# GDN inverse with tiles of 32 weight columns, first value tile's taps at the iteration's tail, SSD state groups one step later

## The reference, cut to what matters

```python
# GDN, per pair of value heads that share a query and key head (16 such pairs)
qkv = silu(causal_conv(qkv, conv_buf, conv_w))      # 4 taps per channel
a_mat = (k_beta @ k.T) * decay * strict             # lower triangular, per chunk
t_mat = inverse(eye + a_mat)                        # used for u and w of the chunk
# then: new values, state update, output, rmsnorm(o) * silu(z)

# SSD, per group (8 groups of 8 heads): conv, y_diag, state per chunk, y_off, and for the samples
S = S * exp(dt * A) + outer(x * dt, B);  y = S @ C  # 8 sample states per group
```

## Time and profile before

| what | value |
|---|---|
| time, median of 3 runs (lowest to highest) | 2444.06 us (2442.49 to 2444.54) |
| the profiled execution's own time | 2443.26 us |
| its span, first to last instruction | 2441.5 us |
| mean granted clock of TensorE, share of full | 0.990 |
| PE / DVE / ACT / POOL busy | 96% / 66% / 52% / 72% |
| one iteration of the GDN loop | 63.5 us (L440 at 286.05 and at 349.58) |

### The profile page before, as it was taken

How to read it: one execution, slowest core, us unless ns; L and a number is a source line. 1 busy time by engine, 2 the same in 40 slices (tenths; PEclk the granted TensorE clock), 3 DMA queues, 4 the chain that set the end, 5 groups by cost and what they waited for, 6 DMA issues and landing times.

```text
span 2441.5 us, 58796 instructions
## 1 busy us (share of the span) xinstructions
PE 2346.2 (96%) x21280; PEld 2201.1 (90%) x21280; DVE 1604.1 (66%) x3203; ACT 1260.5 (52%) x2201; POOL 1762.6 (72%) x2236
## 2 busy tenths in 40 slices
PE   5899999999999999999998989999999999999997
PEld 5799999999999999989998978989998999899897
DVE  7667666666666676661217466988898889712374
ACT  4555555555555555543335446555555555433443
POOL 5466566565555555558887968988898889789896
PEclk9999999999999999999999989999999999999998
DMA  5444444444444444436443445766576656554433
GB/s 200 149 156 148 155 155 148 151 142 148 144 155 147 148 143 143 146 114 222 155 164 134 163 152 204 239 202 202 189 240 212 198 193 229 189 182 155 155 136 123
DMA packets 126772, 410.84 MB, mean 168 GB/s; under 512 B 21344, under 2 KB 37984, under 8 KB 122112
## 3 DMA queue, kind: packets, MB, share of 16 engines
q1 hardware_dynamic: 80784, 294.49, 35.3%
q10 hardware_dynamic: 45936, 115.64, 14.0%
HBM read 363.47 MB, written 46.61 MB: 168 GB/s over the span
## 4 chain that ended last, share of the span: by engine, by line
PE 53%; POOL 32%; issue 10%; DVE 3%; ACT 1%; POOLq 0%; DMA 0%; DVEq 0%; ACTq 0%
POOL wl L335 32%; PE psj L358 14%; PE psj L359 12%; PE psj L360 12%; PE psA L393 2%; PE psC L393 2%; PE psE L393 2%; PE psD L504 1%; PE psA L569 1%; PE psC L519 1%; DVE xl L1398 1%; PE psA L382 1%; PE psE L535 0%; PE psE L387 0%; PE psC L387 0%
## 5 line engine op out<-in xcount | busy, mean ns | idle before, releaser
L335 POOL TENSOR_TENSOR wl<-ring,wh 128x256 fp32r<-128x256 f32 x2232 | 1762.4, 822 | 656.2 <-ACT wh L806 651.8
L358 PE MATMUL psj<-xh,wh 128*128 128x288 f32 x4400 | 1358.0, 309 | 37.2 <-DVE xl L1413 17.0
L359 PE MATMUL psj<-xl,wh 128*128 128x288 f32 x4400 | 1305.1, 297 | 0.0
L360 PE MATMUL psj<-xh,wl 128*128 128x288 f32 x4400 | 1300.3, 296 | 0.0
L358 PEld LDWEIGHTS psj<-xh,wh 128*128 128x128 f32 x4400 | 831.4, 189 | 90.9 <-issue 52.7
L806 ACT ACTIVATE wh<-ring 128x1024 fp32r<-128x1024 f32 x558 | 586.1, 1059 | 596.1 <-PE psj L360 556.9
L359 PEld LDWEIGHTS psj<-xl,wh 128*128 128x128 f32 x4400 | 834.2, 190 | 1.9
L360 PEld LDWEIGHTS psj<-xh,wl 128*128 128x128 f32 x4400 | 835.0, 190 | 0.0
L887 ACT ACTIVATE arena<-psj 128x256 f32<-128x256 f32 x112 | 42.8, 383 | 206.7 <-PE psj L360 200.5
L1768 DVE TENSOR_TENSOR h<-h,psj 128x288 f32 x32 | 14.5, 454 | 154.9 <-PE psj L360 154.9
L1839 DVE SCALAR_TENSOR_TENSOR arena<-arena 128x256 f32<-128x256 f32 x144 | 111.3, 799 | 3.4
(11 more groups left out here) (345 smaller groups left out, 2935.5 us busy)
## 6 DMA issues: line engine op xcount, KB each, us to landing
ring<-weights_d SPq DMA_DIRECT2D x558, 512.0 KB, 3.3
h<-gstate_d ACTq DMA_DIRECT2D x16, 1024.0 KB, 6.3
gst_s_d<-h ACTq DMA_DIRECT2D x16, 1024.0 KB, 3.9
h<-sstate_d ACTq DMA_DIRECT2D x32, 512.0 KB, 5.6
sst_s_d<-h ACTq DMA_DIRECT2D x32, 512.0 KB, 4.1
arena<-g_rows_d ACTq DMA_DIRECT2D x16, 864.0 KB, 6.0
arena<-s_rows_d ACTq DMA_DIRECT2D x8, 1152.0 KB, 8.7
h_spill_d<-h ACTq DMA_DIRECT2D x2, 2304.0 KB, 7.2
```

Of the source, the lines that this page charges most:

```text
L335: ins = pool.tensor_tensor(wl[:, s, n:n + 2], ring[:, s, n:n + 2], wh[:, s, n:n + 2].bitcast(F32), ALU.subtract)
L358: pe.matmul(out, w_h, xh[:, kt, :], start=(kt == 0), stop=False)
L359: pe.matmul(out, w_h, xl[:, kt, :], start=False, stop=False)
L360: mm = pe.matmul(out, w_l, xh[:, kt, :], start=False, stop=(kt == KT - 1))
```

## The change

- `blocks` gets the number of weight columns of a product as an argument. For A*D (psC) and for the update of D (psA) it is 32: four products for each matrix, each with 32 weight columns and the same 32 moving columns as before, for 32 rows of the output. For the update of E (psE) it stays 64.
- The prompt taps 0, 1 and 2 of value tile 0 leave the inverse. They are made in `v_first`, behind the norm of the next queries and keys and ahead of the Y writes, after a wait for ScalarE's take of that tile (`took_act` at m * 6 + 11). For the first iteration they are made in the prologue. Tap 0 of value tile 1 goes to the very start of an iteration, ahead of L1544. The other taps move up by one place or more, and `g_convv` is raised ahead of `mask_p(4)`.
- In the 7 iterations of the SSD loop the two groups of state products and the sum go from steps 45, 55 and 70 to 46, 56 and 71. The last iteration stays.

```diff
@@ -80,7 +80,7 @@
 
 SMP_PE = {n: i + 1 for i, n in enumerate(("ast", "sqs", "esp", "smp", "us", "osm"))}
 SMP_ACT = {n: i + 1 for i, n in enumerate(("asc", "kmc", "qs", "vnds"))}
-G_DVE_LINKS, S_DVE_LINKS = 19, 40
+G_DVE_LINKS, S_DVE_LINKS = 16, 40
 S_CONV = ((0, 2), (2, 4), (4, 5), (5, 6))
 ARENA = 15900
 
@@ -387,10 +387,10 @@
                     mm = pe.matmul(bank[r:r + 64, cols], lhsT[:, r:r + 64], rhs, start=True, stop=True)
                 return mm
 
-            def blocks(bank, u, lhsT, rhs, lv):
-
-                for r in (0, 64):
-                    mm = pe.matmul(bank[r:r + 64, u * 32:(u + 1) * 32], lhsT[:, r:r + 64], rhs[:, in_block(r, lv), :],
+            def blocks(bank, u, lhsT, rhs, lv, n):
+
+                for r in range(0, P, n):
+                    mm = pe.matmul(bank[r:r + n, u * 32:(u + 1) * 32], lhsT[:, r:r + n], rhs[:, in_block(r, lv), :],
                                    start=True, stop=True)
                 return mm
 
@@ -455,7 +455,7 @@
                     for u in range(4):
                         D = half(gDE[:, 0], lv, 0)[:, u]
                         if lv < 5:
-                            mm = blocks(psC, u, gAT[:, u, :], D, lv)
+                            mm = blocks(psC, u, gAT[:, u, :], D, lv, 32)
                         else:
                             mm = halves(psC, slice(u * 64, (u + 1) * 64), gAT[:, u, :], D)
                     mm.then_inc(S("g_p"), 1)
@@ -466,12 +466,12 @@
                     pe.wait_ge(S("g_pm"), m * 6 + lv + 1)
                     if lv < 5:
                         for u in range(4):
-                            mm = blocks(psA, u, gDE[:, 1, u, :], half(gP[lv], lv, 0)[:, u], lv)
+                            mm = blocks(psA, u, gDE[:, 1, u, :], half(gP[lv], lv, 0)[:, u], lv, 32)
                         mm.then_inc(S("g_qd"), 1)
                     for u in range(4):
                         E = half(gDE[:, 1], lv, 1)[:, u]
                         if lv < 5:
-                            mm = blocks(psE, u, gP[lv][:, u, :], E, lv)
+                            mm = blocks(psE, u, gP[lv][:, u, :], E, lv, 64)
                         else:
                             mm = halves(psE, slice(u * 64, (u + 1) * 64), gP[lv][:, u, :], E)
                     mm.then_inc(S("g_qe"), 1)
@@ -683,7 +683,7 @@
 
             def ssd_mix(m, e, more):
 
-                at_smp, at_xt, at_states, at_sum = (33, 36, (45, 55), 70) if more else (41, 46, (54, 62), 72)
+                at_smp, at_xt, at_states, at_sum = (33, 36, (46, 56), 71) if more else (41, 46, (54, 62), 72)
                 if e == 20:
                     pe.wait_ge(S("s_cv"), m + 1)
                     pe.wait_ge(S("s_yd"), m + 1)
@@ -1536,8 +1536,22 @@
                 dve.tensor_tensor(gATS[:, :, :], gDTS[0:NS], gR[0:NS, :, 1, SEQ:T], ALU.mult)
                 do.link(dve.tensor_tensor(u4(gAT[:, :, :]), u4(gDT[:, :, :]), beta, ALU.mult))
 
+            def v_tap(i, j, part):
+
+                a, b, at = ((0, SEQ, j), (SEQ, T, UC + DEC_B * j))[part]
+                out = gCR[:, 2 + i, a:b]
+                return dve.scalar_tensor_tensor(out, gU[:, 2 + i, at:at + b - a], gpc_tap[1][:, i, j:j + 1],
+                                                out, ALU.mult, ALU.add)
+
+            def v_first():
+
+                do.link(v_tap(0, 0, 0))
+                do.link(v_tap(0, 1, 0))
+                v_tap(0, 2, 0)
+
             def gdn_body(m, full):
 
+                v_tap(1, 0, 0)
                 dve.wait_ge(S("g_tok"), m + 1)
                 kk = bc(psC[:, 0:256].rearrange("p (c t) -> p c t", c=NC), 2, 2)
                 qk = bc(psC[:, 256:512].rearrange("p (c t) -> p c t", c=NC), 2, 2)
@@ -1559,13 +1573,6 @@
                                             bc(gKN[:, 1 - n, SEQ:T].rearrange("p (t b) -> p t b", b=DEC_B), 1, DEC_B),
                                             bc(seq_mask, 2, DEC_T), ALU.mult)
                 ins.then_inc(S("g_mk"), 1)
-
-                def v_tap(i, j, part):
-
-                    a, b, at = ((0, SEQ, j), (SEQ, T, UC + DEC_B * j))[part]
-                    out = gCR[:, 2 + i, a:b]
-                    return dve.scalar_tensor_tensor(out, gU[:, 2 + i, at:at + b - a], gpc_tap[1][:, i, j:j + 1],
-                                                    out, ALU.mult, ALU.add)
 
                 def parts(lv):
                     return [(slice(r, r + 64), in_block(r, lv)) for r in (0, 64)] if lv < 5 else [(slice(0, P), slice(0, 1))]
@@ -1602,30 +1609,26 @@
                 dve.wait_ge(S("g_e1"), m + 1)
                 do.link(dve.tensor_copy(gU[:, 2:4, UC:US], gpc_cache[1]))
                 mask_p(0)
-                do.link(v_tap(0, 0, 0))
+                v_tap(1, 1, 0)
                 less_q(0)
                 do.link(v_tap(0, 0, 1))
                 mask_p(1)
-                do.link(v_tap(1, 0, 0))
+                v_tap(1, 2, 0)
                 less_q(1)
-                v_tap(1, 0, 1)
-                do.link(v_tap(0, 1, 1))
+                do.link(v_tap(1, 0, 1))
                 mask_p(2)
-                do.link(v_tap(0, 1, 0))
+                v_tap(0, 1, 1)
                 less_q(2)
-                do.link(v_tap(1, 1, 0))
+                do.link(v_tap(1, 1, 1))
                 mask_p(3)
                 dve.wait_ge(S("g_sample_pe"), m * 6 + SMP_PE["sqs"])
                 dve.tensor_tensor(gBS[:, :, :], bc(ident[0:NS, 0:NS], 1, 2),
                                   psD[0:NS, 256:256 + 2 * NS].rearrange("p (j t) -> p j t", j=2), ALU.add) \
                     .then_inc(S("g_bs"), 1)
-                do.link(v_tap(0, 2, 0))
                 less_q(3)
-                v_tap(1, 2, 0)
-                do.link(v_tap(1, 1, 1))
-                mask_p(4)
                 v_tap(0, 2, 1)
                 v_tap(1, 2, 1).then_inc(S("g_convv"), 1)
+                mask_p(4)
                 dve.wait_ge(S("g_sample_pe"), m * 6 + SMP_PE["esp"])
                 dve.tensor_copy(gES,
                                 bc(psD[0:2 * NS, 320:320 + NS], 1, 4)) \
@@ -1708,6 +1711,8 @@
                 states(3)
                 if full:
                     gdn_qk_norm(m + 1)
+                    dve.wait_ge(took_act, m * 6 + 11)
+                    v_first()
                 else:
                     take_out(T_O1, 2)
                 dve.wait_ge(S("g_ont"), m + 1)
@@ -1742,6 +1747,9 @@
             columns(0)
             gdn_prepare(0)
             dve.wait_ge(took_act, 6)
+            do.link(v_tap(0, 0, 0))
+            do.link(v_tap(0, 1, 0))
+            do.link(v_tap(0, 2, 0))
             with dve.Fori(0, GH - 1) as m:
                 do.enter(m, G_DVE)
                 gdn_body(m, True)
```

## The result

| kernel | us, median (lowest to highest) | against before |
|---|---|---|
| before | 2444.1 | |
| the change | 2514.9 (2511.7 to 2519.4) | 1.0294 [1.0278, 1.0309], slower |

The forecast was 2467 with a range of 2440 to 2492: the sign was right, the size wrong by three times (+71 instead of +23). The profiled execution of the changed kernel took 2519.4 us, with a span of 2517.6.

The account below looks back on a forecast made before the run. PE was taken as the bound, busy for 96% of the span. The terms summed as 2443.3 - 20 + 37 + 2 + 10 - 4.5 - 1 = 2467 us, with a range of 2440 to 2492.

Parts of the forecast that it names:

- part 1: GDN inverse levels: psC and psA products in tiles of 32 columns gain 0.25 us a level, -20 us in all.
- part 2: GDN tail taps delay VectorE: PE waits about 2.5 us at L440 in 15 iterations, +37 us; first iteration +2.
- L603's 9 ns: Time per record of 32 weight and 32 moving columns at L603, basis for 8.5 ns a record in the tile groups.
- the 0.12 of drain: Time in us on PE from a group's last record to the next tile shape, added to psC's and psA's groups.
- the rival that priced a record at 27 ns: Inverse's psC and psA groups: records of 32 columns cost 27 ns as at L504, about 2540 us in all; chance 5%.
- the 25 ns floor: PE products: a page's start-to-start minimum, by which a group of 32 would last 0.8 us and the tiles lose.
- +10 of clock: PE behind the L440 stalls: half of 15 stalls bring a half-speed stretch losing 1.7 us each, +10 us.
- nothing: GDN tail: ScalarE's work queued behind g_y moves from 340 to 344, its users over 6 us later, so no cost.
- Part 3: SSD loop: state groups a step later end the 0.67 us wait at L753 for 7 groups, -4.5 us.
- the last iteration: Last GDN iteration: taps end before mask_p(4), so ScalarE's silu and the split of Y start about 1 us sooner, -1 us.
- A deeper stall: GDN loop: g_y misses PE's 344.05 or levels 1 and 2 wait, every stall brings half clock; 2491 us, chance 15%.

Follow-up runs that it names:

- the kernels of 5 and 6: Whole change (2449.4 us), and the same with the taps left as before (2417.2 us), both with PE's GDN loop starting on a packet's first slot and a prefetch hint.

## Why the prediction was wrong

**The step that failed** is one the sum hadn't got: in part 1, "after the change both groups have 32 records" was priced as time on PE only. 160 more product records in the loop's code are, with their weight loads, 320 more instructions, and these were never held against what before's loop needs. The whole change measures 2449 to 2452 where only the fetches are taken away, so they cost about 64 of the 71 us. The terms that the sum did have are too high as well: without fetches they should give 2467, 15 to 18 more than measured. That is mostly part 2: 49 were forecast for the taps, and the kernels of 5 and 6 that differ by them alone are 32 apart. Without this second error the forecast would have been still further from 2515. The page of before had the clue to the fetches: 35 packets in all, none between 222 and 1000 us, so the loop was resident, at 1484 instructions and, by the estimate of 1546, with 62 to spare.

**Part 1, the tiles (-20).** Right as far as it went. Timeline of PE in after, against the earlier trace rows:

```profile
320.70 0.46 PE L393 MATMUL psA<-arena 128*32 128x32 f32 x32
321.09 0.66 PE L393 MATMUL psE<-arena 128*64 128x32 f32 x16
```

```profile
377.67 0.46 PE L393 MATMUL psC<-arena 128*32 128x32 f32 x32
378.07 0.40 PE L358 MATMUL psj<-xh,wh 128*128 128x288 f32 x1
```

Both groups take 0.39 to 0.40, as worked out from L603's 9 ns and the 0.12 of drain (psA slightly better than the 0.41 to 0.44). An iteration without a jump is 1.43 shorter with the tiles alone (said: 1.25); times 16 that is 23. With it falls the rival that priced a record at 27 ns; the 25 ns floor of "TensorE: Matmul & The Clock Gate" (the Trainium skill, Back-to-back issue gap), which was weighed there, doesn't hold for these 32 records in 0.46 us.

**Part 2, the taps (+37, +2 and +10 of clock).** VectorE came as late at its tail as said. Taps only, timeline of DVE, against the earlier trace rows; to compare, take off 9.1 us (L431 stands at 353.15, in the earlier trace rows at 344.05):

```profile
349.25 2.90 DVE L1543 SCALAR_TENSOR_TENSOR arena<-arena 128x256 f32<-128x256 f32 x3 [3.46 <-ACT arena L888]
352.08 0.74 DVE L1719 SCALAR_TENSOR_TENSOR Y<-psE,prm,arena 128x512 f32 x1
...
352.93 0.54 DVE L1532 COPY arena<-arena 128x16 f32<-128x16 f32 x1
353.39 0.15 DVE L1533 COPY arena<-arena 128x2 f32<-128x2 f32 x1
...
354.44 0.67 DVE L1537 TENSOR_TENSOR arena<-arena 128x512 f32<-128x512 f32 x1
355.93 0.78 DVE L1543 SCALAR_TENSOR_TENSOR arena<-arena 128x256 f32<-128x256 f32 x1 [0.82 <-ACT arena L888]
356.63 0.67 DVE L1558 TENSOR_TENSOR arena<-arena,psC 128x512 f32<-128x512 f32 x1
```

The taps begin at 340.15 by before's clock (said: 340.24), Y at 342.98 (342.9). Then it parts: the preparation ends at 346.0, not 347.8. This is the term of part 2 that was too large. Its two small copies take 0.54 and 0.15 here, where before they took 0.78 each beside a busy GpSimd; timeline of DVE, before:

```profile
339.49 0.78 DVE L1532 COPY arena<-arena 128x16 f32<-128x16 f32 x1
340.19 0.78 DVE L1533 COPY arena<-arena 128x2 f32<-128x2 f32 x1
```

GpSimd has nothing to do for 1.35 us of this preparation. I had written "nothing" for ScalarE's being queued behind g_y; but the upper halves that GpSimd works on are queued there too. POOL in the same stretch:

```profile
354.80 4.35 POOL L335 TENSOR_TENSOR wl<-ring,wh 128x256 fp32r<-128x256 f32 x5 [1.35 <-ACT wh L806]
```

Against that, the tap ahead of L1558 waits 0.82 for ScalarE's second take, which I had left out. L1558 (before's L1544) starts 1.9 late instead of 3.4, and PE waits 0.88 at L440 and 0.45 at psA. An iteration is 1.68 us longer and the clock has no dip (1.00 over 353 to 368), where 2.5 us and another 0.67 us (10 over 15) lost to the clock were forecast. The first iteration's wait at L440 grew by 3.7 (9.0 against 5.3), where 2 was forecast. Alone the part costs 26, not 49. In the change as it is, it shows only at the first L440 and at the one behind the loop's exit (0.88), since PE's own standstills cover it. Without fetches it costs 2.0 to 2.2 an iteration beside the tiles; that this is more than 1.68 because the levels are shorter there is argued, not tested.

**Part 3 and the last iteration (-4.5, -1).** From the last iteration's L440 to the end of the span after is 5.5 us shorter than before (1387.6 against 1393.1), and the waits at L753 fell from 5.1 to 0.4. For the SSD steps the forecast is right (4.5 alone). The -1 of the last iteration isn't shown: with the taps only that same stretch takes 1394.2, so 1.1 longer than before.

**Rivals.** "A deeper stall" (2491) and the 27 ns (2540) lie about equally far from 2515, one under and one over it, and both for another cause: the groups take 0.40, and PE never waited at L431, where it asks for g_y. No rival spoke of code length, so no chance was given to what happened.

## What to carry over

Count an edit's instructions as well as its time: a loop that is longer than the engine keeps pays at every jump, here 5 to 10 us an iteration with 1644 or 1804 instructions where 1532 cost next to nothing. The first sign is the packet count of the instruction queue: in the trace of before it is zero inside the loop, which says that the loop is resident and may stop being so. If the loop is over, try the hint on the closing branch and the loop's place before giving up the edit. And judge parts of a change by the iteration without the new stall: standstills of one engine hide the lateness of another.

## What the runs showed of the hardware

- PE's loop of 1772 instructions stays resident if it starts with a packet, one of 1568 that starts some 10 before a packet's end doesn't always (fetches at 4 of 14 jumps); 1804 from a packet's start are fetched in every iteration, and with the prefetch hint in none.
- A fetched packet of 16 KB takes about 1 us (5.8% of 16 engines over 1 us), but it comes later beside data: with 1 MB of states issued 1.3 us ahead of the compare (tiles only) it started 3.1 to 5.4 us after the compare, and 0.9 to 1.4 after it where the states were issued later (the change, and the tiles with the late load).
- 32 product records with 32 weight columns take 0.39 to 0.40 us with the drain, whether psE's or psj's products follow. 48 idle waits cost 0.01 us in an iteration of 63.54; with 84, the iterations without a fetch take 63.55.
